# The last stage of a hybrid decoder step with seven half-size products for each 1024x1024 product

## The reference

```python
def layer_out(h, gates, o_c, o_s, o_w, y_conv, p_l, out_norm, w_out, norm_mlp, w_up, w_down,
              norm_ple, w_ple_gate, w_ple_proj):
    o_att = (gates[:, :, 0, ..., None] * o_c + gates[:, :, 1, ..., None] * o_s
             + gates[:, :, 2, ..., None] * o_w).reshape(B, T, ATT_WIDTH)
    mix = jnp.concatenate([rmsnorm(o_att, out_norm[:ATT_WIDTH]),
                           rmsnorm(y_conv, out_norm[ATT_WIDTH:])], axis=-1)
    h = h + mix @ w_out
    h = h + jnp.square(jax.nn.relu(rmsnorm(h, norm_mlp) @ w_up)) @ w_down
    h = h + jax.nn.sigmoid(rmsnorm(h, norm_ple) @ w_ple_gate) * (p_l @ w_ple_proj)
    return h
```

## Time and profile before

| | us |
|---|---|
| median of 3 runs | 4495.2 (4488.69 to 4501.18) |
| the profiled execution | 4493.93 |
| its span, first to last instruction | 4492.1 |
| `prompt`, from its first query load to its last output sum | 1108.8 to 1934.9 |
| `tail`, from its first DMA to the end of the span | 2158.5 to 4492.1 |
| PE busy | 4032.9 (90%) |
| DVE, ACT, POOL busy | 1124.8, 800.1, 206.9 |

### The profile page before, as it was taken

The page is one execution under the profiler, slowest core; times in us unless marked ns, Lnnn a source line. Parts: engine busy times, 40 slices in busy tenths (PEclk is TensorE's granted clock), DMA queues, the critical chain, the costliest instruction groups (busy, mean ns, idle before and its releaser), DMA issues.

```text
span 4492.1 us, 63082 instructions
## 1 busy us (share of the span) xinstructions
PE 4032.9 (90%) x24550; PEld 3424.1 (76%) x24550; DVE 1124.8 (25%) x2811; ACT 800.1 (18%) x1553; POOL 206.9 (5%) x253
## 2 busy tenths in 40 slices
PE   8999995444899999945799999999999999999999
PEld 6888884444677777735688888888888888888888
DVE  4344331102766555510110003100021000210001
ACT  1100000000666666610100001100011000110000
POOL 0010000000100000000100000000000000000000
PEclk9999997767999999965799999999999999999999
DMA  4101007665111110022332222322223222222221
GB/s 159 43 12 50 24 15 240 193 188 164 27 20 18 16 13 9 6 57 57 113 113 75 75 75 94 113 79 75 75 94 113 75 75 77 90 81 77 75 75 66
DMA packets 214144, 348.16 MB, mean 78 GB/s; under 512 B 41383, under 2 KB 141536, under 8 KB 212713
## 3 DMA queue, kind: packets, MB, share of 16 engines
q1 hardware_dynamic: 162328, 292.76, 20.7%
q10 hardware_dynamic: 50697, 43.79, 3.2%
q0 software_dynamic: 864, 7.85, 0.5%
HBM read 312.51 MB, written 36.56 MB: 78 GB/s over the span
## 4 chain that ended last, share of the span: by engine, by line
PE 51%; DMA 0%; POOL 0%; ACT 0%; SPq 0%; DVE 0%; issue 0%; ACTq 0%; POOLq 0%
PE ps_t L1547 26%; PE ps_t L1571 25%; PE ps_hs L1540 0%; DMA w_ring<-in_w_tail 0%; POOL h_square_sum L1681 0%; SPq L1489 0%; ACT L1631 0%; DVE ff L1716 0%; ACT h_square_sum L1631 0%; ACT h_square L1635 0%; DVE ff L1722 0%; DVE h L1723 0%; SPq L1486 0%; SPq L1485 0%; SPq L1478 0%
## 5 line engine op out<-in xcount | busy, mean ns | idle before, releaser
L1571 PE MATMUL ps_t<-h_gained,w_ring 128*128 128x257 f32 x5120 | 1111.2, 379 | 0.0
L1571 PEld LDWEIGHTS ps_t<-h_gained,w_ring 128*128 128x128 f32 x5120 | 966.0, 189 | 143.8
L1547 PE MATMUL ps_t<-ff,w_ring 128*128 128x257 f32 x4096 | 888.5, 379 | 0.0
L1547 PEld LDWEIGHTS ps_t<-ff,w_ring 128*128 128x128 f32 x4096 | 772.8, 189 | 115.1
L319 PE MATMUL ps_z<-x_gained,w_in_sb 128*128 128x257 f32 x2816 | 620.4, 380 | 21.2 <-DVE x_gained L355 21.2
L319 PEld LDWEIGHTS ps_z<-x_gained,w_in_sb 128*128 128x128 f32 x2816 | 532.9, 189 | 103.2 <-issue 22.3
L958 ACT ACTIVATE PT_pr<-ps_p 128x384 f32<-128x384 f32 (+4 forms) x576 | 256.4, 497 | 220.9 <-PE ps_p L905 200.4
L1707 DVE SCALAR_TENSOR_TENSOR ff<-ps_t,rstd_h 128x514 f32<-128x514 f32 x128 | 88.8, 694 | 785.5 <-PE ps_t L1571 785.5
L569 PE MATMUL ps_cmp<-pages,w_cmp_sb 128*64 128x128 f32 x2048 | 147.6, 318 | 119.9 <-DMA pages<-in_cache_cmp 119.9
L940 ACT ACTIVATE S_pr<-S_pr,nmax_pr 128x640 f32<-128x640 f32 (+15 forms) x256 | 251.1, 982 | 21.8 <-DVE nmax_pr L1053 19.7
L1547 PE MATMUL ps_t<-mix_chunk,w_ring 128*128 128x257 f32 x1024 | 230.8, 387 | 26.0 <-DMA w_ring<-in_w_tail 23.3
(11 more groups left out here) (244 smaller groups left out, 2536.4 us busy)
## 6 DMA issues: line engine op xcount, KB each, us to landing
w_ring<-in_w_tail SPq DMA_DIRECT2D x328, 512.0 KB, 3.4
pages<-in_cache_cmp SPq DMA_DIRECT2D x256, 128.0 KB, 3.3
pages<-in_cache_cmp ACTq DMA_DIRECT2D x256, 128.0 KB, 3.7
w_in_sb<-in_w_in SPq DMA_DIRECT2D x22, 512.0 KB, 13.9
x_chunk<-in_xT SPq DMA_DIRECT2D x16, 514.0 KB, 7.0
mix_chunk<-scratch_mixT SPq DMA_DIRECT2D x4, 2056.0 KB
x_chunk_t<-in_xT SPq DMA_DIRECT2D x4, 2056.0 KB
out_yT<-h SPq DMA_DIRECT2D x32, 257.0 KB
```

The source lines that it names most:

```text
L1547: mm = pe.matmul(zp[zi][:, hh, 0:HF], w[:, i], src[:, k, hh * HF:(hh + 1) * HF], start=(first and i == 0), stop=(final and i == len(ks) - ...
L1571: mm = pe.matmul(zp[m % 3][:, hh, 0:HF], w[:, k], a[:, k, hh * HF:(hh + 1) * HF], start=(k == 0), stop=(k == KT - 1), skip_group_check=True)
```

## The change

**What is computed.** Each 1024x1024 product C = W A, with A a chunk's 1024x514 activations, is cut into quarters: W into four 512x512 blocks, A into four of 512x257. Seven products of a 512x512 block by 512x257 columns replace eight. Four of the seven stationary operands and three of the seven moving operands are sums of quarters, and the four quarters of C are sums of the seven products. `tail_plan` lists 160 "pairs" (kind, chunk, group, m): ten products x four chunks x four output tiles m of 128 rows in either half. A pair has seven pieces, P1 to P7, of four multiplications each (K = 512).

**The tail.** The MLP runs in four groups of 1024 hidden features (up 0, up 1, down 0, up 2, down 1, up 3, down 2, down 3), and `ff` has two buffers. Six PSUM banks (`ps_tx`, `ps_ty`, `ps_tz`, two each) hold the pieces. P3 and P4 of a pair come behind P1 and P6 of the next one, except at the end of out and of down 3, where two parts of the projection stand before P3 and two behind P4 (none at out in chunk 0, whose projection opens the stage). ACT copies P1 to SBUF; DVE makes every sum that reads PSUM (`p1`, `u2`, `u3`) and takes the results; GpSimd adds three of the four quarters to `h` and makes the operand sums of `ff` (`ff_sums`); DVE makes those of `h_gained` (`h_sums`) and of `mix`. Nothing loops in hardware any more. A piece's weights are one ring unit of 256 KB (16 slots); there are 1136 units. The norm of the attention half is made before the first multiplication of out.

**The weight sums.** Four sums of weight quarters for each of 40 (product, m) go to a DRAM scratch tensor `w_sums`. GpSimd makes them in `prompt`, two or three at a time behind the `mix_bias` of each query tile, four 128x512 additions each (`weight_sums`); SP loads 1 MB for each (`load_w`) and stores 1 MB (`store_sums`), and its program has these ahead of the gate and query loads of that tile. An item's load is issued behind the store of the item before it.

```diff
+W_AT_ONCE = 2
+W_ITEMS = [(b, m) for b in range(10) for m in range(4)]
+W_SHARE = [range(len(W_ITEMS) * q // NT, len(W_ITEMS) * (q + 1) // NT) for q in range(NT)]
...
+                def store_sums(n):
+                    sp.wait_ge(s_wd, 4 * n + 4)
+                    sp.dma_start(d["w_sums"][W_ITEMS[n]].rearrange("s p n -> p s n"), t["w_blocks"][:, n % W_AT_ONCE]).then_inc(
+                        s_ws[n % W_AT_ONCE], 16)
+                    if 1 <= n < len(W_ITEMS) - W_AT_ONCE + 1:
+                        sp.wait_ge(s_ws[(n - 1) % W_AT_ONCE], 16 * ((n - 1) // W_AT_ONCE + 1))
+                        load_w(n - 1 + W_AT_ONCE)
...
                 for q in range(NT):
+                    for n in W_SHARE[q]:
+                        store_sums(n)
                     if q + 2 < NT:
                         sp.wait_ge(s_oo, other_at["cmp", q] + 1)
                         load_gate(q + 2)
...
+                def weight_sums(n):
+                    pool.wait_ge(s_wl[n % W_AT_ONCE], 16 * (n // W_AT_ONCE + 1))
+                    a11, a12, a21, a22 = (t["w_blocks"][:, n % W_AT_ONCE, i] for i in range(4))
+                    own.post(pool.tensor_tensor(a22, a21, a22, ALU.add), s_wd, 1)
+                    own(pool.tensor_tensor(a21, a11, a21, ALU.subtract), s_wd, 1)
+                    own(pool.tensor_tensor(a11, a22, a11, ALU.subtract), s_wd, 1)
+                    own.post(pool.tensor_tensor(a12, a12, a11, ALU.subtract), s_wd, 1)
...
+                    for n in W_SHARE[q]:
+                        weight_sums(n)
...
+def tail_plan():
...
+    steps, behind = [("proj", 0, i) for i in range(4)] + [("sums", 0, "att")], None
+    for j, (kind, c, g, m) in enumerate(pairs):
+        steps += [("P1", j), ("P6", j)]
+        if m == 0 and (kind == "gate" or (kind, g) == ("up", 0)):
+            steps.append(("sums", c, kind))
+        if behind is not None:
+            steps += [("P3", behind), ("P4", behind)]
+        steps += [("P5", j), ("P2", j), ("P7", j)]
+        behind = j
+        if (kind, g, m) == ("down", 3, 2) and c < 3:
+            steps.append(("sums", c + 1, "att"))
+        if m == 3 and (kind == "out" or (kind, g) == ("down", 3)):
+            first = 4 * (kind == "down")
+            fill = [("proj", c, first + i) for i in range(4)] if first or c else []
+            steps += fill[:2] + [("P3", j), ("P4", j)] + fill[2:]
+            behind = None
...
+                def project(s):
...
+                        if aux[s] + hh >= 2:
+                            pe.wait_ge(s_ax, aux[s] + hh - 1)
...
+                def product(name, j):
...
+                    w = weights(n)
+                    ready(name, j)
...
+                    if name == "P2":
+                        pe.wait_ge(s_p1, j + 1)
+                    if name == "P7":
+                        pe.wait_ge(s_u2, j + 1)
+                    if name == "P4":
+                        pe.wait_ge(s_u3, j + 1)
+                    if name == "P3":
+                        pe.wait_ge(s_c22, j + 1)
...
+                    for k in range(4):
+                        if name in ("P6", "P5", "P4"):
+                            b = tsum[:, {"P5": 0, "P6": 1, "P4": 2}[name], k]
+                        else:
+                            b = quarter(src, {"P1": "11", "P2": "21", "P3": "22", "P7": "12"}[name], k)
+                        mm = pe.matmul(bank[:, 0:HF], w[:, k], b, start=(name in ("P1", "P6", "P5") and k == 0),
+                                       stop=(name in ("P2", "P4", "P3") and k == 3), skip_group_check=True)
+                    mm.then_inc(s_wu, 1)
...
+                    elif name == "P7":
+                        used(dve, s)
+                        if j >= 2 and pairs[j - 2][0] != "up":
+                            consumed(dve, j - 2, "22")
+                        own(tt(U3[:, p], P1[:, p], bY[p][:, 0:HF], ALU.add), s_u3, 1)
+                        own(tt(U3[:, p], U3[:, p], bZ[p][:, 0:HF], ALU.add), s_c22, 1)
+                        if kind in ("up", "gate"):
+                            own.post(shaped(j, "22", U3[:, p]), after(kind), 1)
```

698 lines of the change are left out of this document (450 added, 248 removed).

## The result

The changed kernel takes **4286.7 us** (median of 4 runs, 4279.8 to 4295.5) against 4491.9 us for the kernel before on the same chip: a ratio of 0.954, 95% interval 0.952 to 0.957. The profiled execution takes 4288.2 us with a span of 4286.3 us. The forecast was 4247 us with a range of 4217 to 4305. So the sign and the mechanism hold, and 40 us of the forecast gain are missing: the time lies above the 4217 to 4275 that had a chance of 0.70, and inside the range only because that was drawn out to the price of rival A. Two questions remain: where the 40 us went, and why.

The account below looks back on a forecast made before the run. PE's multiplications were taken to bound the tail. 2186.5 + 2000 + 25.5 + 10 + 6.5 = 4228.5, plus 15 for attention gives a 4243.5 us span, 4245.3 profiled, 4247 median; range 4217 to 4305.

Parts of the forecast that it names:

- rival A: Prompt attention pays 58 us more: GpSimd's additions meet DVE's on the path, more tiles late; 4305 us, chance 0.12.
- Part 1: Tail products: 4480 PE multiplications instead of 5120 at 0.434 us each, saving 278 us; short pieces cost nothing extra.
- Part 2: Tail, work beside PE: 3 us late at each of seven places; 25.5 us with chunk 0's out and the ends.
- Part 3: Start of the tail: out begins at about 2186.5, PE idling 7 us before it; 10 us for clock and restarts.
- Part 4: Sum of the tail: 2000 us of PE after 2186.5, plus 25.5, 10 and 6.5 us, gives 4228.5.
- Part 5: Tail weight loads: 1136 units of 256 KB, one every 1.74 us, sixteen ahead; taken to cost 0.
- Part 6: Prompt attention with the weight sums: 15 us longer, from 160 GpSimd additions and the items' loads and stores.
- the chain: Prompt attention: items' loads, sums and stores delay biases and gates, mainly at query tiles 2 to 4; 10 us.
- DVE beside the additions: Prompt attention: DVE operations stretched while a GpSimd addition runs; between 0 and 58 us, taken as 5.
- B: Tail's regular stretch hands over late, 160 pairs each waiting 0.3 us: 48 us more, 4295 us, chance 0.10.
- C: Ring's weight loads bound the tail, slower than before: at 2.1 us a unit 409 us more, 4656, chance 0.03.
- D: Tail saving doesn't appear because a piece's multiplication is not 0.434 us; time within 0.3% of before, chance 0.01.

Follow-up runs that it names:

- copies-first run: Changed kernel with ACT copying a projection part's two banks before the gain of the piece ahead, at fourteen places: 4258.5 us.
- run with the sums early: Kernel with weight sums in the first stage and ACT's projection copies ahead of gains, plus mix's small sum of squares before half the first chunk's projection: 4202.8 us.
- run with four units: Changed kernel with 4 units of weights loaded ahead in the last stage instead of 16: 4313.6 us.
- its parts: Two runs against the changed kernel: item loads and stores without the additions, 4244.8 us; the additions without those transfers, 4282.0 us.
- items given out late: Changed kernel with whole additions, but no weight-sum items at query tiles 0 to 4 and more at later tiles: 4272.4 us.
- with parts: Changed kernel with no items at tiles 0 to 4 and each GpSimd addition made as four of 128x128: 4252.7 us.

## Why the prediction was right, and where 40 us were wrong

**Part 1** held: 8960 records, 1.73 to 1.74 us a piece, no pair late but two.

**Part 2** had the place, and the copies-first run shows that the order of ACT's program is the cause. The term was 21 us for the fourteen waits and measured 28.3. At the second parts PE waits 1.84 us where I had put 1.6; at the first parts it waits 2.2 us where I had put 1.4 (my own terms add up to 1.2). What the term left out there is DVE's queue: in all seven places the sums of `h_gained` stand ahead of P7's two sums and hold them up by 1.3 us, of which 0.9 is L1912 beside GpSimd's sum of squares, so the exclusion reaches into the tail as well. From DVE's first sum to PE's start it is 2.6 us, less than the 2.9 that I had put with the hand-overs. With the other waits the term is 33.1 instead of 25.5.

**Part 3:** 28.3 us from the first DMA to out against 28. Inside it PE waits 14.7 us for its first weights and 7.8 us for the norm; out begins 2.5 us later than it need, because the whole projection stands ahead of the sums, as the run with the sums early shows.

**Part 4:** PE's own time from there on is 2015.5 us (2056.3 less 33.1 of waits and 7.7 of end), against 2010; 2 us of the difference are a slip of mine, 4480 x 0.434 is 1944 and not 1942. The tail as a whole is 14.6 us over, half of it from part 2.

**Part 5** held with room to spare, as the run with four units shows.

**Part 6** is where the 35 us were lost. Its two terms were 10 us for the chain and 5 us for DVE beside the additions. The chain was sized right: 10 us are left between the changed kernel and its parts, and DVE's waits for a gate and the biases, which the term was worked out for, are 9.4; they are gone with the items given out late. The other term measured 35 to 40. The step that failed is the reason given for taking 5 between 0 and 58: "most DVE work reads PSUM and waits for PE anyway". It counted DVE's time, where the number and the place of its operations decide. 240 additions, products and scalar operations work on SBUF alone, 75 us in all, most of about 0.2 us and many of them between two steps that PE or ACT wait for: a chunk's maximum before the exponentials, the coefficients before PE spreads them. One that meets an addition waits for half of it on average, however short it is itself (0.65 of 1.30 us). Three numbers, 240 operations, 0.23 of the time (187 of 826 us) and half of 1.17 us, would have given an estimate of 32 us. The one row that I looked at, L1011 with one stretched of 16, was the wrong sample: GpSimd had 75 us of work in that stage then, and has 282 now. The sum with 35 more, 14.6 for the tail and -6.5 (the stage begins 3.9 us earlier and the sample stage ends 2.6 us faster in this execution) gives 4288, the profiled time. The 4286.7 us lie in the range by the room left for rival A, not because Part 6 was right.

The Trainium skill's rule (SBUF — State Buffer, section Who interferes with whom), which I had set against this part, is borne out: DVE's operations with two inputs in SBUF are shut out by GpSimd instructions that read SBUF, by copies as well as by additions. The same section lets `tensor_scalar` in a 2-port mode contend and says that reductions do not; L1044 went from 213 to 414 ns, and in the row at 1773.40 a reduction keeps its 0.16 us. By that rule with every addition meeting one operation I had worked out 53 us more; about 35 came.

**The rivals.** A is what happened in its first half, the additions on the path, at 35 of the 58 us that it had over the forecast; the chain did not grow. (With the 5 us already taken, A's price would have been 53 us, as by the rule.) B did not: two waits in 160 pairs. C did not: no wait for `w_ring` behind the first. D did not.

## What to carry to other kernels

Before work is put on an idle engine, count the short operations of the engine that shares memory access with it, take the share of time it will be busy and half the length of one of its instructions, and multiply: that is an estimate of what the busy chain pays, whatever the busy sums say. Here it fitted three runs within 4 us and was 8 to 11 us too high in three. The same work costs nothing in a stage where the engine that is disturbed has slack (the first stage here), and much less in short instructions. In an engine's program, put the copy that frees a bank ahead of work whose input comes later.

## What the runs showed of the hardware

- DVE's additions and scalar operations from SBUF to SBUF on 2 to 32 columns, 0.16 to 0.2 us by themselves, took up to 1.30 us beside GpSimd additions with a median of 1.27 us. Reductions, maxima and reciprocals kept their time (reciprocals 203 ns), and so did additions and products with one input from PSUM (128x512: 691 and 692 ns with items and without). GpSimd is held up as well: its additions have a median of 1271 ns and a maximum of 1807, and that longest one begins at 1391.73, 0.01 us behind a DVE addition of 0.69 us.
- GpSimd pays for each instruction: 455 ns for an addition of 128 columns, 1271 for 512. An estimate from the two: 2.1 ns a column and 0.18 us that do not go away.
- Two kernels that are alike up to there go through the first tile of the attention at different clocks. The late items with whole additions, then with parts (no item in either yet; clock in the last field but two):

```profile
1120.21:1146.55 26.34, 24.60 (x122) 13.33 (x122) 14.30 (x62) 13.73 (x56) 2.90 (x9) 0.50 0.41 106
```

```profile
1117.92:1140.42 22.50, 19.33 (x122) 10.57 (x122) 14.37 (x63) 13.58 (x56) 2.90 (x9) 0.73 0.49 115
```

  At 1.2 GHz throughout (0.50) the tile takes 3.8 us longer. Differences of up to 5 us between the attention stages of these runs are of this kind. What sets the clock at that point no run shows.
- GpSimd's own DMA queue carried 80 loads and 80 stores of 512 KB in the first stage, 84 MB in 590 us or 142 GB/s (168 with the stage's other transfers), each at about 0.77 us of GpSimd's time, landing after 5.2 us (loads) and 3.5 us (stores).
